# Dense experts by whole-table streaming in place of gathered expert rows

## The reference

```python
q = (xc @ w_q).reshape(t, PEER_HEADS, 2, PEER_QDIM // 2)
sc = jnp.einsum('thpc,hpnc->thpn', q, sub_keys)
v_half, i_half = lax.top_k(sc, 16)
cand = (v_half[:, :, 0, :, None] + v_half[:, :, 1, None, :]).reshape(t, 8, -1)
cand_idx = (i_half[:, :, 0, :, None] * 128 + i_half[:, :, 1, None, :]).reshape(t, 8, -1)
top_s, pos = lax.top_k(cand, 16)
expert = jnp.take_along_axis(cand_idx, pos, axis=-1)
g = jax.nn.softmax(top_s, axis=-1)
act = gelu(einsum('thkd,td->thk', u_tab[expert], xc))
return einsum('thk,thkd->td', g * act, v_tab[expert])
```

## Time and profile before

| | us |
|---|---|
| median of 3 runs | 2111.54 (2107.38 to 2118.32) |
| the profiled execution, its span | 2111.6 |
| TensorE busy | 1648.0 |
| VectorE busy | 1375.4 |
| GpSimd busy | 1128.4 |
| ScalarE busy | 388.8 |
| bytes moved by DMA | 720.79 MB |

### The profile page before, as it was taken

One profiled execution on the slowest core, in us unless ns is written; L12 is line 12 of the kernel. 1 busy time (PEld: TensorE's weight loads), 2 busy tenths in 40 slices (PEclk: granted clock), 3 DMA queues, 4 the chain that ended last, 5 costly groups with the idle time before them and its releaser, 6 DMA issues.

```text
span 2111.6 us, 15758 instructions
## 1 busy us (share of the span) xinstructions
PE 1648.0 (78%) x4610; PEld 828.8 (39%) x4610; DVE 1375.4 (65%) x3269; ACT 388.8 (18%) x902; POOL 1128.4 (53%) x1028
## 2 busy tenths in 40 slices
PE   3997999998567978987876888878768996555565
PEld 1465887444233434432343433333434442111111
DVE  6564432142796695687757668776784887777775
ACT  1022000012121222222122222221322221100001
POOL 0000000000377577577766767776687777777773
PEclk9977999998789979999796999999788999887667
DMA  9851569162799999999999999999999999999997
GB/s 357 303 197 60 165 194 329 57 238 80 245 372 385 401 399 407 401 406 380 400 396 406 404 403 406 408 397 401 397 354 384 407 394 365 408 409 409 409 410 313
DMA packets 254483, 720.79 MB, mean 341 GB/s; under 512 B 24518, under 2 KB 49598, under 8 KB 253886
## 3 DMA queue, kind: packets, MB, share of 16 engines
q0 software_dynamic: 147456, 536.94, 65.0%
q1 hardware_dynamic: 106942, 182.85, 24.2%
HBM read 718.66 MB, written 1.05 MB: 341 GB/s over the span
## 4 chain that ended last, share of the span: by engine, by line
PE 40%; DMA 21%; POOL 17%; DVE 13%; issue 7%; ACT 2%; SPq 0%; POOLq 0%; DVEq 0%; ACTq 0%
POOL gring L1699 17%; DMA gring<-in_peer_v_dram,sel_idx 17%; PE PS L621 13%; PE PS L753 7%; PE PS L825 5%; PE PS L826 5%; DVE gring L1537 4%; PE PS L727 4%; PE PS L566 3%; DMA gring<-in_peer_u_dram,sel_idx 2%; DMA wring<-in_hyb_w_in_dram 1%; DVE xs L1556 1%; PE PS L670 1%; PE PS L687 1%; PE PS L706 1%
## 5 line engine op out<-in xcount | busy, mean ns | idle before, releaser
L1699 POOL DMA_INDIRECT gring<-in_peer_u_dram,sel_idx x512 | 566.0, 1105 | 725.1 <-DVE sel_g L1523 556.2
L825 PE MATMUL PS<-gring,diags 128*128 128x512 f32 x736 | 449.0, 695 | 321.3 <-DMA gring<-in_peer_v_dram,sel_idx 211.5
L1699 POOL DMA_INDIRECT gring<-in_peer_v_dram,sel_idx x512 | 562.2, 1098 | 230.3 <-issue 130.5
L1537 DVE CUSTOM_DVE_ANT_0 gring<-gring,hs 128x1024 f32<-128x1024 f32 x400 | 482.1, 1221 | 134.3 <-DMA gring<-in_peer_u_dram,sel_idx 133.1
L826 PE MATMUL PS<-gring,diags 128*128 128x512 f32 x736 | 434.2, 676 | 0.0
L621 PE MATMUL PS<-wring,hTs 128*128 128x512 f32 (+3 forms) x968 | 410.4, 574 | 9.8 <-DVE hTs L1125 4.3
L825 PEld LDWEIGHTS PS<-gring,diags 128*128 128x128 f32 x736 | 135.4, 210 | 545.4 <-issue 383.4
L621 PEld LDWEIGHTS PS<-wring,hTs 128*128 128x128 f32 x968 | 179.8, 195 | 219.8 <-issue 217.4
L826 PEld LDWEIGHTS PS<-gring,diags 128*128 128x128 f32 x736 | 158.8, 216 | 210.5 <-issue 210.5
L1063 ACT ACTIVATE diags<-consts,acts 128x128 f32<-128x128 f32 x368 | 136.4, 397 | 511.3 <-PE PS L826 476.8
L1537 DVE CUSTOM_DVE_ANT_0 gring<-gring,PS 128x1024 f32<-128x1024 f32 x112 | 136.4, 1220 | 70.4 <-DMA gring<-in_peer_u_dram,sel_idx 70.4
(11 more groups left out here) (194 smaller groups left out, 1188.9 us busy)
## 6 DMA issues: line engine op xcount, KB each, us to landing
wring<-in_peer_w_q_dram SPq DMA_DIRECT2D x32, 1024.0 KB, 14.7
wring<-in_w_ada_dram SPq DMA_DIRECT2D x24, 1024.0 KB, 9.7
wring<-in_w_up_dram SPq DMA_DIRECT2D x44, 512.0 KB, 5.1
wring<-in_hyb_w_in_dram SPq DMA_DIRECT2D x20, 1024.0 KB, 8.3
wring<-in_w_in_dram SPq DMA_DIRECT2D x10, 1024.0 KB, 8.1
wring<-in_hyb_w_out_dram SPq DMA_DIRECT2D x8, 1024.0 KB, 19.2
gring<-in_peer_u_dram,sel_idx POOLq DMA_INDIRECT x512, 12.9
gring<-in_peer_v_dram,sel_idx POOLq DMA_INDIRECT x512, 13.4
```

Of the source, the lines that this page charges most:

```text
L825: pe.e.matmul(ybank[0], d, row[i % NG][:, 0:512], start=first, stop=last)
L1537: e.tensor_tensor_reduce(row[i % NG], row[i % NG], hbank if (l, t) == (1, 1) and hd else h[t], 1.0, 0.0, ALU.mult, ALU.add, acts[:, c:c + ...
L1699: gp.e.indirect_dma_start(out=row[i % NG], out_offset=None, in_=table, in_offset=bass.IndirectOffsetOnAxis(ap=sel_idx[:, c:c + 1], axis=0) ...
```

## The change

**Tables are streamed whole.** For each layer SyncE loads, into the same ring of six slots, 64 blocks of `u` (`us` steps; two first keys each, 256 experts, 1 MB) and then 64 blocks of `v` (`vs` steps). The `u` table is given to the program in another layout, with the model dimension on partitions. The indirect gathers, the GpSimd program and `gring` as a row ring go.

**Up.** A `us` step is 16 products 128x256: stationary a 128x128 block of `u`, moving the turned rows `hc` of both token tiles. ScalarE applies Gelu to the 512 columns and writes them to `big` (16384 experts x 256 tokens, 128 KB a partition). `gring`, `keep`, `hs`, `hTs` and `work` now are parts of `big` and are not to be had while it is full.

**Gates.** `pick` leaves first keys, second keys and gates in `sel`; `et` turns them. For each group of 8 tokens, VectorE makes one-hot matrices of the second keys (128x1024) and of the first keys, times the gate (two 128x512 operations), in the double buffer `hots`; TensorE multiplies them (`scat`, 8 products of 64 columns, one a token), which sums the gates over the choices of a token at their place among 64 first x 128 second keys; VectorE multiplies that onto the Gelu values in `big`. There are two halves of 64 first keys, 32 groups each: the first is mixed with the second half of the up steps, the second with the first half of the down steps.

**Down.** A `vs` step is, for each token tile, 4 products 128x512: stationary the 128 experts x 128 tokens of `big`, moving 512 columns of `v`. They accumulate over all 128 blocks in two PSUM banks a tile.

**Order.** Layer by layer: hybrid tile 1 is merged with the choice of tile 0; then the experts of both tiles, whose first 32 up steps are merged with the choice of tile 1; then MLA tile 0 alone; MLA tile 1 with the choice of tile 0; the experts of layer 1. The second norm gains come in as columns at the start (`columns`), where they were three broadcast loads.

The core of the diff:

```diff
-    c00 = choose(0, 0)
...
-    together(16 + 32 * 7, PACE[0], c00, hybrid(1), choose(1, 0))
-    together(16 + 32 * 8, 16.0, left.pop())
-    together(16 + 32 * 15, PACE[1], mla(0), choose(0, 1))
-    together(16 + 32 * 16, 16.0, left.pop())
-    together(16 + 32 * 23, PACE[2], mla(1), choose(1, 1))
-    together(16 + 32 * 24, 16.0, left.pop())
...
+    gather(0, 0)
+    merge(chunks(hybrid(1)), chunks(choose(0, 0)), 0.9)
+    gather(1, 0)
+    put("et", 0, 0)
+    put("hT", "c10")
+    put("hTe", "c10")
+    experts(0, chunks(choose(1, 0)))
+    merge(chunks(mla(0)), [])
+    gather(0, 1)
+    merge(chunks(mla(1)), chunks(choose(0, 1)), 0.9)
+    gather(1, 1)
+    put("et", 0, 1)
+    put("hT", "c11")
+    put("hTe", "c11")
+    experts(1, chunks(choose(1, 1)))
```

and in `experts`:

```diff
+        merge(chunks(dense(l)), second, 0.85)
+        put("hot", l, 0, 0)
+        for n in range(NP // 2):
+            put("us", l, NP // 2 + n)
+            if n + 1 < NP // 2:
+                put("hot", l, 0, n + 1)
+            put("scat", l, 0, n)
+        put("hot", l, 1, 0)
+        for n in range(NP - TAIL):
+            put("vs", l, n, 0)
+            if n < NP // 2:
+                if n + 1 < NP // 2:
+                    put("hot", l, 1, n + 1)
+                put("scat", l, 1, n)
+            put("vs", l, n, 1)
+        for t in range(2):
+            for n in range(NP - TAIL, NP):
+                put("vs", l, n, t)
+            put("xadd", l, t)
```

TensorE's new steps (the waits of the first down step are left out):

```diff
+            def up_expert(l, n):
...
+                        for i0 in (0, 4):
+                            ready(("hT", f"c{t}{l}", i0))
+                b, ps = take(("us", l, n), "act")
+                uw = wring[:, 2048 * s:2048 * s + 2048].rearrange("p (j k m) -> p j k m", j=2, k=8)
+                for j in range(2):
+                    for k in range(8):
+                        ins = pe.e.matmul(ps[:, 256 * j:256 * j + 256], uw[:, j, k, :], hc[:, k, :], start=(k == 0),
+                                          stop=(k == 7))
+                ins.then_inc(full[b], 1)
+                w_free[("us", l, n)] = (full[b], filled[b])
...
+            def scatter(l, half, g):
+                pe.wait_ge(hot, hot_n[(l, half, g)])
+                b, ps = take(("scat", l, half, g), "vec")
+                one, two = hot_bufs(g)
+                for i in range(8):
+                    ins = pe.e.matmul(ps[:, 64 * i:64 * i + 64], two[:, i, :], one[:, i, :], start=True, stop=True)
+                ins.then_inc(full[b], 1)
+
...
+            def down_expert(l, n, t):
...
+                pe.wait_ge(w_landed[s], landed)
+                vw = wring[:, 2048 * s:2048 * s + 2048].rearrange("p (j d) -> p j d", j=2)
+                for j in range(2):
+                    w = moes[:, first_key(n) + j, 128 * t:128 * t + 128]
+                    for c in range(2):
+                        b = vbanks[t][c]
+                        ins = pe.e.matmul(PS[:, 512 * b:512 * b + 512], w, vw[:, j, 512 * c:512 * c + 512],
+                                          start=(n, j) == (0, 0), stop=(n, j) == (NP - 1, 1))
+                        if (n, t, j) == (NP - 1, 1, 1):
+                            ins.then_inc(full[b], 1)
```

VectorE's:

```diff
+                first, second, gates = (m[:, at:at + 8].unsqueeze(2) for m in pickedT(t))
+                if g >= 2 or half:
+                    arrived(("scat", l, half, g - 2) if g >= 2 else ("scat", l, 0, 30 + g))
+                there(("et", t, l, 0))
+                keys = iota128[:, 64 * (1 - half):64 * (1 - half) + 64].unsqueeze(1).to_broadcast([128, 8, 64])
+                done(e.tensor_tensor(two, second.to_broadcast([128, 8, 128]),
+                                     iota128.unsqueeze(1).to_broadcast([128, 8, 128]), ALU.is_equal))
+                ve.wait_ge(*done(e.tensor_tensor(one, first.to_broadcast([128, 8, 64]), keys, ALU.is_equal)))
+                e.tensor_tensor(one, one, gates.to_broadcast([128, 8, 64]), ALU.mult).then_inc(hot, 1)
...
+            def scatter(l, half, g):
+                ps = arrived(("scat", l, half, g))
+                there(("us", l, 31 + 32 * half))
+                dst = moes[:, 64 * (1 - half):64 * (1 - half) + 64, 8 * g:8 * g + 8]
+                freed(("scat", l, half, g), e.tensor_tensor(dst, ps.rearrange("p (t i) -> p i t", t=8), dst, ALU.mult))
```

SyncE's:

```diff
+            def up_expert(l, n):
+                s, _ = w_at[("us", l, n)]
+                sp.wait_ge(*w_free[w_before[("us", l, n)]])
+                i = first_key(n)
+                uw = wring[:, 2048 * s:2048 * s + 2048].rearrange("p (j m) -> p j m", j=2)
+                sp.e.dma_start(uw, a["peer_u_t"][l, i:i + 2].rearrange("j p m -> p j m")).then_inc(w_landed[s], 16)
+
```

More of the change, by code:

```diff
@@ L170, in hybrid @@
         put("obT", "hy", t)
+        if not t:
+            for step in (("sq", "g1"), ("norm", "g1"), ("add", "g1"), ("sq", "h1"), ("norm", "h1")):
+                put(*step)
         yield from projection(("hyo", t), (t,))
@@ L198, in choose @@
     def choose(t, l):
[L199 to L206, removed]
+        if not t:
+            put("hT", f"c{t}{l}")
+            yield 1.0
+            put("hTe", f"c{t}{l}")
+            yield 1.0
         put("keys", t, l)
@@ L217, in choose @@
                 put("mm", ("wq", t, l), (t,), g, k0, t)
-                yield 3.4
-                for _, units in zip(range(4), picking):
-                    yield units
             put("qturn", t, l, g)
+            yield 3.4
+            yield from picking
             picking = pick(g)
[L223 to L256, removed]
+        yield from picking
+        if t:
+            put("et", t, l)
+    def dense(l):
+        for n in range(NP // 2):
+            put("us", l, n)
+            yield
@@ new lines, in chunks, with merge @@
+    def chunks(gen):
+        out, at = [], len(steps)
+        for units in gen:
+            out.append((units or 1.0, steps[at:]))
+            del steps[at:]
+        out.append((0.0, steps[at:]))
+        del steps[at:]
+        return out
+    def merge(a, b, over=1.0):
+        total_a, total_b = sum(u for u, _ in a), sum(u for u, _ in b) / over
+        done_a = done_b = 0.0
+        a, b = list(a), list(b)
+        while a or b:
+            if a and (not b or done_a / total_a <= done_b / total_b):
+                units, part = a.pop(0)
+                done_a += units
+            else:
+                units, part = b.pop(0)
+                done_b += units
+            steps.extend(part)
@@ L258, in order, with gather @@
+    def gather(t, l):
+        put("sq", f"c{t}{l}")
+        put("norm", f"c{t}{l}")
     hy = hybrid(0)
@@ L262, in order @@
                 pass
-    c00 = choose(0, 0)
[L264 to L270, removed]
-    together(16 + 32 * 7, PACE[0], c00, hybrid(1), choose(1, 0))
-    together(16 + 32 * 8, 16.0, left.pop())
-    together(16 + 32 * 15, PACE[1], mla(0), choose(0, 1))
-    together(16 + 32 * 16, 16.0, left.pop())
-    together(16 + 32 * 23, PACE[2], mla(1), choose(1, 1))
-    together(16 + 32 * 24, 16.0, left.pop())
-    put("sq", "fin0")
-    put("norm", "fin0")
-    upto(10 ** 6)
-    put("sq", "fin1")
-    put("norm", "fin1")
+    gather(0, 0)
[13 more added lines that the diff above has]
+    experts(1, chunks(choose(1, 1)))
+    for t in range(2):
+        put("sq", f"fin{t}")
+        put("norm", f"fin{t}")
     return steps
@@ L371, in program @@
                  for key, i in HELD.items()]
-        row = [gring[:, D * i:D * (i + 1)] for i in range(NG)]
-        gain = late + [gring[:, 13 * D:14 * D]]
+        gain = [gring[:, D * i:D * (i + 1)] for i in (9, 10, 11, 13)]
+        final_gain = hots[:, 0:D]
         cw = keep[:, 0:128]
@@ L377, in program @@
         cwT = keep[:, 256:344]
-        cwT_and_norms = keep[:, 256:368]
         ones = keep[:, 384:512]
```

399 lines of the change are left out of this document (179 added, 220 removed).

## The result

The changed kernel took 3110.36 us (median; 3109.02 to 3110.91) against 2111.54 for the kernel before in the same measurement (the median of three runs; a fourth took 5494.56 us and is left out), a ratio of 1.473 [1.469, 1.476]. The profiled execution's span is 3107.2 us. The forecast of 3018 us had the direction and the size. The range of 2930 to 3200 us held the time, and 89 us (3%) of the span were missing from the sum.

What follows compares the result with a forecast made beforehand. Before, TensorE was taken as the bound up to 517.7 us and DMA after; changed, TensorE bounds the expert layers. Front 518 + middle stages 440 + expert layers 2050 + end 10 = 3018 us, range 2930 to 3198.

Steps and rivals of the forecast that it cites:

- The bound and the bytes: Whole kernel: DMA stops being the bound, bytes fall to about 452 MB, the stream asks about 152 GB/s, transfers cost nothing.
- rival 3: Expert stages: table loads no faster than 14.7 us one after another, 3763 us there, 4730 in all; 2%.
- Up and down: Expert stages, TensorE per layer: up 443 us at 0.433 a product, down 439 us at 0.858.
- Rival 2: Expert layers: dense work does not keep the clock, 0.90 granted, 228 us more, 3245 us; 5%.
- rival 4: Expert products: one row of each pair goes, so up, down and scatter halve, 2034 us, 3.7% faster; 1%.
- Scatter: Gate products on TensorE: 0.20 us each, bounds 0.17 and 0.27, 102 us per layer (87 to 137).
- Choice of tile 1 and joints: Up half: choice adds 36 us of TensorE with its 65 us of VectorE hidden; joints 5 us.
- The cover: Expert stages: VectorE's 3.4 us a one-hot group hides behind TensorE's 8.5 us, as does ScalarE's Gelu.
- Middle stages: Mixers, with tile 0's choices, between expert layers: 157 + 9, 120 and 145 + 9 us, together 440; bounds 380 and 550.
- rival 1: Middle stages: VectorE and TensorE wait head by head and the clock falls, 550 to 620 us, total 3130 to 3200; 15%.
- The check by busy time: Whole kernel, the sum another way: TensorE busy 1648.0 - 883.2 + 2 x 984 = 2733 us, plus idle time.
- the missing cover: MLA tile 0 alone: nothing covers ScalarE's softmax, so 120 us, beside hybrid tile 0's 106 us.

## Why the prediction was right, and where it was off

The differences of the stages, measured less predicted, make up the missing 89 us: front 517.0 - 518, hybrid tile 1 with choice 188.6 - 166, MLA tile 0 104.6 - 120, MLA tile 1 with choice 205.3 - 154, two expert layers 2 x (1041.5 - 1025), end 8.6 - 10; -1 + 23 - 15 + 51 + 33 - 1.

- **The bound and the bytes: right.** 452.05 MB moved for 452 predicted, at 145 GB/s for about 150, loads landing in 4.9 us. Half the load changed nothing, so costing transfers at nothing was right, and rival 3 is out.
- **Up and down: right.** 0.435 and 0.865 us a product for 0.433 and 0.858 predicted. Taking the pace of dense stretches, and not the mean of 381 or 594 ns a row, was what made this work: two rows of 594 ns would have given 1.19 us a product. Rival 2 is out by PEclk 1.00 over 1041.5 us, rival 4 by 4096 and 2048 rows for 2048 and 1024 products.
- **Scatter: a term mis-sized.** 0.216 us a product instead of 0.20, 110.6 us a layer instead of 102, 17 us in both. I had two prices, 0.17 from two rows at full clock and 0.27 from twelve products at a lower clock, and took the value nearer to the two rows, which was too little to rest on. By the Trainium skill ("TensorE: Matmul & The Clock Gate", section on LDWEIGHTS) an estimate is 0.213 us for two loads of 128 columns. The trace agrees within 2%, and the run with 32 columns supports the reason. In bf16 the trace does not agree with that rule: 0.03 us a product, load included (0.24 us for eight).
- **Choice of tile 1 and joints: right in size.** A group takes 10.05 us under the up steps (four are 40 us, 36 predicted); what is left of the up half's 544.8 us is 4 us of joints, of which 2 are the low clock of the first 16 up products (9.05 us for 6.96).
- **The cover: right.** The expert products waited for VectorE only for 1.8 us before the first up products and 2.0 us at the passages from up to down. The bf16 runs show where it ends: at a pace of 3.06 us a group.
- **Middle stages: the step that failed.** Two things were wrong in it. The first is the overlap. I took "two queues of nearly equal load that wait for each other in order" and still let them overlap, 157 us for 110 and 105. They hardly overlap. Hybrid tile 1 alone takes 121 us and the choice put behind it 74 (195.4 in all); merged they take 188.6. In layer 1 the merge even costs 11 us. The cause is what rival 1 named, waiting for each other head by head; the measured 499 us lie between the 440 of the sum and the 550 from which rival 1 starts. Doubling part of the picks showed it from the side of the cause. The second is TensorE's load. VectorE's came out as priced (106.75 and 96.17 us busy for 105 and 95), but TensorE was busy for 143.33 and 143.95 us where I had 110 in both, and for 142.45 us in layer 0 unmerged as well. So even complete hiding would have left hybrid tile 1 with the choice at some 143 us at its granted clock of 0.79. The check by busy time had the same gap: 2906.2 us for 2733. MLA tile 0 alone took 105 us, as long as hybrid tile 0's 106: the 14 us that I added for the missing cover were not needed, and by luck they took 15 us off the miss.

What stays open is how much of the mixers' 347 us (121 + 226) is the granted clock of 0.77 to 0.83 and how much the waits themselves. Both come together in every run here, and none separated them. That holds for TensorE's 33 us above its price too. Open as well is what another merge would give, with smaller pieces of the pick or the heads' operations put ahead of them: only this one was run.

## What to carry to other kernels

Before trading bytes for products, price the products of that dtype from a dense stretch: here the f32 form of the stream was 47% slower and the bf16 form 16% faster than the f32 gathers, at the price of coarser numbers. If work for another engine is to be hidden, put it beside a long stretch of products that need nothing of that engine; merging it with a chain that crosses the same two queues hid almost nothing here (7 us of the choice's 74 in layer 0, and a loss of 11 in layer 1), since each queue runs in order and the chain waits behind the merged piece. An f32 product with a 128x128 stationary operand cost the same with 64 columns as with 32 (0.216 and 0.213 us): halving its columns gave nothing.

## What the runs showed of the hardware that I had not expected

- An f32 product costs four times a bf16 one in both wide shapes: 0.435 against 0.11 us at 256 columns, and 0.865 against 0.22 at 512 (118 rows of L890 in 25.73 us in the run with bf16). In f32 there are two rows a product, in bf16 one, and each f32 row takes twice the time of a bf16 row. The Trainium skill ("FP8 and Floating Point Precision", section TensorE Precision Notes) counts four passes for true f32, and the trace agrees for these shapes; the row count alone would have suggested two. At 64 columns the factor is seven (0.216 against 0.03 us).
- The granted clock was 1.00 on the mean over two expert layers of 1041.5 us each, with TensorE busy nearly all the time. Only their first microseconds were lower: in layer 0 it was 0.50 (1.2 GHz) from 705.6 to 709.0 us, and the first 16 up products took 9.05 us instead of 6.96; from 714.7 to 1747.1 us it was 1.00 (2.4 GHz). It was 0.79 on the mean in the stage before the first of them, where TensorE was idle for 45 of 188.6 us.
- ScalarE converts a block of 128x2048 from f32 to bf16 in 1.91 us and was not the bound at one block per 2.5 us.
- VectorE idle for 44% of a stage (busy 106.75 of 188.6 us) was no room for more work: two thirds of what was added there showed (18.8 of 27.8 us).
